# Output projection of the hybrid layer: first column block run whole, recurrence tiles first, retention output put behind the last pair of sparse attention

## The reference, cut to what matters

```python
proj = x @ w_in
y_ret = retention(rq, rk, rv) * silu(rg)            # 256 features
y_nsa = nsa(nq, ...) * silu(ng)                     # 512 features, 8 heads
y_lru = rg_lru(lx, ...) * silu(lg)                  # 256 features
y = concatenate([y_ret, y_nsa, y_lru], -1) @ w_out  # 1024 x 1024
x = layer_norm(ALPHA * x + y)
```

## Time and profile before

| | us |
|---|---|
| median of three runs | 900.06 |
| the profiled execution | 900.72 |
| its span | 898.8 |
| TensorE matmuls busy | 889.1 (99%) |
| TensorE weight loads busy | 766.7 (85%) |
| VectorE busy | 624.4 (69%) |
| ScalarE busy | 489.7 (54%) |
| GpSimd busy | 40.2 (4%) |

### The profile page before, as it was taken

How to read it: one execution, slowest core, us unless ns; L and a number is a source line. 1 busy time by engine, 2 the same in 40 slices (tenths; PEclk the granted TensorE clock), 3 DMA queues, 4 the chain that set the end, 5 groups by cost and what they waited for, 6 DMA issues and landing times.

```text
span 898.8 us, 13855 instructions
## 1 busy us (share of the span) xinstructions
PE 889.1 (99%) x5614; PEld 766.7 (85%) x5614; DVE 624.4 (69%) x1084; ACT 489.7 (54%) x733; POOL 40.2 (4%) x69
## 2 busy tenths in 40 slices
PE   9999999999999999999999999999999999999998
PEld 7987878987878888877999988888877799998886
DVE  5878977879978998685766644456788486664441
ACT  7566736566737755564655543346567465554330
POOL 2600010000000000000000000000000000000000
PEclk9999999999999999999999999999999999999999
DMA  8963254633345578621655565657464266555540
GB/s 294 330 223 107 94 188 146 235 118 118 96 141 187 170 257 232 188 90 48 212 184 187 185 196 177 218 166 229 123 208 125 87 214 213 186 188 191 183 162 24
DMA packets 79455, 155.55 MB, mean 173 GB/s; under 512 B 5656, under 2 KB 7864, under 8 KB 79392
## 3 DMA queue, kind: packets, MB, share of 16 engines
q1 hardware_dynamic: 75200, 142.81, 48.4%
q0 software_dynamic: 4192, 11.85, 4.6%
HBM read 153.54 MB, written 1.11 MB: 172 GB/s over the span
## 4 chain that ended last, share of the span: by engine, by line
PE 83%; DVE 9%; ACT 4%; issue 2%; DMA 1%; SPq 0%; DVEq 0%; ACTq 0%
PE ps L764 17%; PE ps L766 16%; PE ps L765 16%; PE ps L795 8%; PE ps L797 7%; PE ps L796 7%; DVE w_lo L1896 2%; ACT w_hi L1412 1%; DMA w_raw<-in_w_in 1%; PE ps_mid L974 1%; PE ps L1065 1%; PE ps_mid L960 1%; PE ps_mid L990 1%; PE ps_mid L764 1%; ACT y_tok L1539 1%
## 5 line engine op out<-in xcount | busy, mean ns | idle before, releaser
L1896 DVE TENSOR_TENSOR w_lo<-w_raw,w_hi 128x2048 fp32r<-128x2048 f32 x133 | 299.7, 2260 | 145.1 <-ACT w_hi L1412 145.0
L1412 ACT ACTIVATE w_hi<-w_raw 128x2048 fp32r<-128x2048 f32 x133 | 250.9, 1890 | 195.6 <-PE ps L766 143.4
L764 PE MATMUL ps<-w_hi,act_hi 128*128 128x512 f32 (+1 forms) x446 | 178.0, 399 | 0.2
L766 PE MATMUL ps<-w_hi,act_lo 128*128 128x512 f32 (+1 forms) x446 | 171.1, 384 | 0.0
L765 PE MATMUL ps<-w_lo,act_hi 128*128 128x512 f32 (+1 forms) x446 | 170.7, 383 | 0.0
L764 PE MATMUL ps<-w_hi,hid 128*128 128x512 f32 x296 | 116.0, 392 | 0.0
L766 PE MATMUL ps<-w_hi,hid 128*128 128x512 f32 x296 | 115.3, 389 | 0.0
L765 PE MATMUL ps<-w_lo,hid 128*128 128x512 f32 x296 | 115.2, 389 | 0.0
L795 PE MATMUL ps<-act_hi,w_hi 128*128 128x256 f32 x384 | 110.4, 288 | 0.0
L796 PE MATMUL ps<-act_lo,w_hi 128*128 128x256 f32 x384 | 107.7, 280 | 0.0
L797 PE MATMUL ps<-act_hi,w_lo 128*128 128x256 f32 x384 | 107.4, 280 | 0.0
(11 more groups left out here) (375 smaller groups left out, 1241.0 us busy)
## 6 DMA issues: line engine op xcount, KB each, us to landing
w_raw<-in_ffn_w SPq DMA_DIRECT2D x64, 1024.0 KB, 5.4
w_raw<-in_w_in SPq DMA_DIRECT2D x21, 1024.0 KB, 5.6
w_raw<-in_a_w_qkv SPq DMA_DIRECT2D x18, 1024.0 KB, 5.1
w_raw<-in_b_w_qkv SPq DMA_DIRECT2D x12, 1024.0 KB, 5.1
w_raw<-in_w_out SPq DMA_DIRECT2D x8, 1024.0 KB, 4.9
w_raw<-in_b_w_o SPq DMA_DIRECT2D x4, 1024.0 KB, 5.0
w_raw<-in_w_in SPq DMA_DIRECT2D x12, 256.0 KB, 5.5
w_raw<-in_w_in SPq DMA_DIRECT2D x4, 512.0 KB, 3.6
```

The costliest lines, as they stand in the source:

```text
L764: pe.matmul(o, ah, wh, start=first, stop=False)
L766: mm = pe.matmul(o, al, wh, start=False, stop=last)
L1412: act.activation(w_hi[:, c % RING, :, 0:n], w_raw[:, c % RAW, :, 0:n], ACT.Copy).then_inc(w_hi_done, 1)
L1896: dve.tensor_tensor(lo, w_raw[:, c % RAW, :, 0:n], hi.bitcast(F), ALU.subtract).then_inc(w_lo_done, 1)
```

## The change

```diff
-        Y_TILES = [0, 3, 1, 2]
-        Y_ORDER = [0, 1, 6, 7, 2, 3, 4, 5]
+        Y_TILES = [3, 0, 1, 2]
+        Y_ORDER = [6, 7, 0, 1, 2, 3, 4, 5]
...
# TensorE
-                    yield from token_steps(o, 0, (0, 1, 6, 7))
-                    yield from token_steps(o + 1, 0, (0, 1))
+                    yield from token_steps(o, 0, (6, 7))
...
-                between = {6: lambda: compressed_transposes(l), 11: lambda: retention_output(l)}
+                between = {6: lambda: compressed_transposes(l), 11: lambda: retention_output(l), 15: lambda: retained_acts(l)}
...
-                        8: lambda: retention_transposes(l), 14: lambda: retained_acts(l)}
+                        8: lambda: retention_transposes(l)}
...
-                tokens(o, 0, (2, 3))
-                tokens(o + 1, 0, (2, 3, 6, 7))
-                for i in range(2):
-                    tokens(o + i, 0, (4, 5))
+                tokens(o, 0, (0, 1, 2, 3, 4, 5))
+                tokens(o + 1, 0, Y_ORDER)
...
# ScalarE
                 def hook13():
                     splits(b + 4, 0)
+
+                def hook14():
                     take(b + 4, 0)
 
-                def hook14():
+                def hook15():
                     mixed_hi(l, 0)
-                    lru_operand(l)
...
-                              13: hook13, 14: hook14}, ...
+                              12: lambda: lru_operand(l), 13: hook13, 14: hook14, 15: hook15}, ...
...
# VectorE
-                def hook12():
-                    retention_norm(l)
-                    retention_gated(l)
-
                 def hook14():
                     take(b + 4, 0)
+                    lru_operand(l)
+
+                def hook15():
                     mixed_lo(l, 0)
-                    lru_operand(l)
...
-                              10: hook10, 11: hook11, 12: hook12, 13: lambda: splits(b + 4, 0), 14: hook14})
+                              10: hook10, 11: hook11, 12: lambda: retention_norm(l), 13: lambda: retention_gated(l), 14: hook14, 15: hook15})
                 gated_output(l, 0)
                 take(b + 4, 1)
                 mixed_lo(l, 1)
                 gated_output(l, 1)
                 mixed_lo(l, 2)
+                splits(b + 4, 0)
                 splits(b + 4, 1)
...
-                dve.wait_ge(at_hi, ACT0[2 * l + 1] + 2)
+                dve.wait_ge(at_hi, ACT0[2 * l + 1] + 1)
```

More of the change, by code:

```diff
@@ L1776, in hook13 @@
                     splits(b + 4, 0)
+                def hook14():
                     take(b + 4, 0)
-                def hook14():
+                def hook15():
                     mixed_hi(l, 0)
-                    lru_operand(l)
                 units(l, 16, {0: lambda: splits(b + 1, 0), 1: hook1, 2: lambda: splits(b + 1, 1), 3: lambda: splits(b + 2, 0), 5: hook5,
                               6: hook6, 7: hook7, 8: hook8, 9: hook9, 10: lambda: splits(b + 3, 1), 11: hook11,
-                              13: hook13, 14: hook14}, front={4: front4, 6: front6, 8: front8})
+                              12: lambda: lru_operand(l), 13: hook13, 14: hook14, 15: hook15}, front={4: front4, 6: front6, 8: front8})
                 take(b + 4, 1)
```

## The result

The changed kernel takes 907.03 us as the median of four runs (905.48 to 909.81), the kernel before 900.12: a ratio of 1.0076, 95% interval 1.0062 to 1.009. It is slower, as forecast, but by 6.9 us instead of 3.3, and it lies outside the stated range (901.8 to 905.2). The profiled execution is the slowest of the four, 909.81 us with a span of 908.0, 9.1 above the profiled execution of before.

A forecast was written before the change was run, and what follows sets the result against it. TensorE, busy 889.1 of 898.8 us, bounds the kernel. Per layer 1.69 us won, 0.2, 3.05 and 0.09 lost: 1.65 slower, +3.3 over two layers, 903.4 us from 900.06; own range 902.4 to 904.6, reaching 901.8 to 905.2.

The forecast's parts named there:

- The wait at L974: Transposes of unit 14 waiting for VectorE's scaling: scaling the pair first removes the wait, 1.55 us a layer.
- Tile 4 of `o`: Block o in half 0: tile 4 needed at 121.0, its last low part ready at 121.2, a wait of about 0.2 us.
- W3 wanted behind two splits: Start of block o + 1: TensorE stands from 122.6 to 125.65 until VectorE has split W2 and W3, about 3.0 us.
- Half 1, normalization, transfers: After half 0: half 1 starts 1.65 us later, at 131.15; normalization stays hidden by 1.6 us, transfers are hidden too.
- The clock: TensorE's granted clock, 1.000 over the whole span: the new wait could lower it, the trace neither confirming nor excluding that.
- The clock falls in the stall: Rival: block o + 1's 24 matmuls run at the lower clock, 5.4 us a layer, 914.3 us in all; chance 0.03.
- The prediction's own sign of being wrong: Among the signs that would refute the forecast: a row showing a granted clock below 1.00 after the stall.
- The rival's price: Clock rival's cost for block o + 1: 24 matmuls at 0.453 us instead of 0.227, 5.4 us a layer.
- the first rival: Rival that the splits are in time: W3 ends at 123.5, stall 0.9, 0.8 us a layer gained, 898.5 us; chance 0.05.
- its break-even at 123.95: End of W3's split at which a layer neither gains nor loses, 1.65 us earlier than forecast.
- the chain slips further: Rival: retention output or ScalarE's copy comes late for L910; a slip of 1 us past the cover gives 905.4; chance 0.08.

The follow-up runs named there:

- e4: Changed kernel with blocks o and o + 1 interleaved and W2's split between the recurrence's and retention's low parts: 897.16 us, 3.4 below the kernel before.
- e2: Changed kernel with block o + 1 taking tiles 0 to 3 (W2) before 6, 7, 4, 5 (W3) in half 0: 899.61 us, ratio 0.9994.
- e9: Kernel before with only the tile order changed: block o whole, recurrence's tiles and operand first: 902.30 us, ratio 1.0023.
- e5: Kernel before with W3's low part written once more ahead of its real split, to make TensorE wait: 904.29 us, 3.3 above before.
- f2: Changed kernel with 6 unread matmuls between blocks o and o + 1, filling half the wait: 903.96 us, ratio 1.0039.
- e3: Changed kernel with W2 split right behind the retention output instead of after the last low part: 901.72 us, ratio 1.0015.
- f1: Changed kernel run again without edit, to see how often its clock falls: 905.95 us, ratio 1.0056.
- e6: Kernel before with W3's low part written twice more ahead of its real split: 912.95 us, 12.0 above before.
- e1: Changed kernel with 12 unread matmuls between blocks o and o + 1, filling the wait for W3's low part: 905.26 us, ratio 1.0056.
- f3: Kernel before with W3's low part written twice more and 16 unread matmuls in the resulting wait: 909.71 us, 8.6 above before.

## Why the prediction was right or wrong

- *The wait at L974.* Right. The transposes start at 112.06 (112.10 forecast), and block `o` at 116.85 (116.8). e4 gained 3.4 us, which is what the prediction gave for the change with no wait for W3.
- *Tile 4 of `o`.* Right: it starts at 121.19, and 121.0 and a wait of 0.2 were forecast.
- *W3 wanted behind two splits.* Right. The wait is 2.84 us in both layers (3.0 forecast) and ends at 125.68 (125.65). It is the order of tiles against the order of splits: with W3 wanted four tiles later (e2) the loss is gone, and in the kernel before, with its splits where they were, the order of tiles costs 1.3 us (e9).
- *Half 1, normalization, transfers.* Hidden, as forecast: L901 follows the start of half 1 by 6.13 us as before, and no other wait of size appeared in the changed kernel. Less the 2.8 us of the clock, half 1 starts at 131.25 (131.15 forecast).
- *The clock.* Wrong. This is the step that failed: the sum has no term for the clock, and busy times were to stay unchanged, where TensorE's grew from 889.1 to 896.0 us. "The clock falls in the stall" stood among the rivals with 0.03, argued away by "the waits of 1.4 us left no mark". That row bore on waits of 1.4 us, and e5, f2 and e3 confirm it for waits up to 1.5. It said nothing of one twice as long. In its place the runs showed two falls worth 5.6 us in the profiled execution. The prediction's own sign of being wrong, a granted clock below 1.00 after the stall, came true. Of the four 2.8 us waits in the two profiled executions of the changed kernel three brought the clock down. The rule of the Trainium skill (TensorE: Matmul & The Clock Gate, Part 1), that TensorE falls to 1.2 GHz once it has been idle, named this outcome. The trace of after agrees with it (0.50 in the wait and behind it), and it had been given almost no weight.
- *A row that was passed over.* The trace of the kernel before does hold a standstill of that length, at its end. TensorE's last matmul ends at 895.61, and the granted clock falls at about 898.4 (the mean of 0.75 over the last 0.8 us), 2.8 us later. "No wait of 3 us in mid-kernel is in the trace" is true, but this row gave a reason to weigh the clock.

```profile
895.22 0.39 PE L766 MATMUL ps<-w_hi,hid 128*128 128x512 f32 x1
...
898.00:898.80 0.80, 0.00 (x0) 0.00 (x0) 0.00 (x0) 0.00 (x0) 0.00 (x0) 0.75 0.00 0
```

- *The rival's price.* 5.4 us a layer is about twice what was measured: the clock came back after thirteen matmuls, not twenty-four, and they started 0.427 us apart, not 0.453. The measured 2.8 us a full fall, 5.6 in all, and 3.3 from the waits, are 8.9 of the 9.1 us between the two profiled executions. The median holds less, since not each wait brings a long fall (f1).

What the waits alone cost is near what was forecast: 2.9 us in f2 and 2.4 in the one run of f1 at a clock of 1.000, against 3.3. So the direction and the waits were no luck; the size was off by the clock. Two sizes in the prediction don't follow from its own terms. For W3 at 123.5 the first rival gives 0.8 us a layer and 898.5 us; by its break-even at 123.95 it is 0.45 a layer, so 899.2. And the stated range ends at 905.2 without a working, below the 905.4 of its rival "the chain slips further". Neither bears on what went wrong.

## What to carry to other kernels

When operands are consumed in an order, list for each wait what it counts, and compare that order with the producer's queue: here a counter made "tile 6 first" mean "both splits first", and moving two tiles behind four others was worth 5.8 to 7.8 us. When an edit makes TensorE stand longer than any row of the trace shows it standing, price the clock as a term of its own with a real chance, since rows of shorter waits say nothing of it, and look at the end of the trace too, where TensorE has stopped. Whether several short waits are cheaper than one long wait of the same sum was not tested; in e3 three of 0.5 to 0.7 us left the clock alone. A growing busy time with the same number of matmuls is the sign to look at the granted clock.

## What the runs showed of the hardware

- Standstills of TensorE of up to 1.5 us in mid-kernel left the clock at 1.00 in every trace. Of the four of 2.84 us, one left it, two brought it to 0.50 some 2.0 us after the last matmul, while TensorE stood, and one about 1.35 us after the wait. Those of 3.76 us did so in both layers of e6's trace, and all four runs of e6 have a mean clock of 0.994.
- The delay isn't fixed. Behind the last matmul of the whole kernel, with no TensorE work after it, the clock fell after about 2.0 us in f2's trace (899.64 to 901.6) and 2.8 in that of before; in that of the changed kernel it was still at 1.00 at the end of the span, 3.2 us later (904.83 to 908.0). So a standstill of 2.84 us can end before the fall or after it. What sets the delay was not found.
- At the lower level 512-column matmuls start 0.427 us apart (0.227 at the upper). The level lasted 3.4 us (f1, and e6 in the first layer) to 6.8 us (the changed kernel), and one fall cost 1.6 to 2.8 us on top of the wait.
- Matmuls whose results nobody reads held the clock up through a wait of either length (e1, f3), but won nothing over an order without the long wait (e2, e4).
